# An SSD loop on one Trainium2 core: ScalarE evicts a projection behind the next tile's exponential and rounds weight chunks by halves

## The reference, cut to what matters

```python
lmat = jnp.exp(jnp.where(mask, seg, -jnp.inf))        # seg = a_cs[l] - a_cs[s]
cb = jnp.einsum('bclgn,bcsgn->bcgls', cc, bc)
y_diag = jnp.einsum('bcgls,bcghls,bcsghp->bclghp', cb, lmat, xdt)
states = jnp.einsum('bclgn,bcghl,bclghp->bcghpn', bc, decay_states, xdt)
# scan over chunks: s = s * chunk_decay + states
y_off = jnp.einsum('bclgn,bcghpn,bcghl->bclghp', cc, prev, jnp.exp(a_cs))
```

## Time and profile before

| what | us |
|---|---|
| median of 3 runs | 3088.34 (3086.95 to 3089.32) |
| the profiled execution, its own time | 3097.28 |
| its span, first to last instruction | 3095.4 |
| TensorE busy | 2751.9 (89%) |
| VectorE busy | 1479.2 (48%) |
| ScalarE busy | 964.9 (31%) |
| GpSimd busy | 656.9 (21%) |

### The profile page before, as it was taken

How to read it: one execution, slowest core, us unless ns; L and a number is a source line. 1 busy time by engine, 2 the same in 40 slices (tenths; PEclk the granted TensorE clock), 3 DMA queues, 4 the chain that set the end, 5 groups by cost and what they waited for, 6 DMA issues and landing times.

```text
span 3095.4 us, 34166 instructions
## 1 busy us (share of the span) xinstructions
PE 2751.9 (89%) x13390; PEld 1402.8 (45%) x13390; DVE 1479.2 (48%) x2307; ACT 964.9 (31%) x1115; POOL 656.9 (21%) x202
## 2 busy tenths in 40 slices
PE   5999988886999999998878787778889899999996
PEld 2577655633444444444454433234444444444443
DVE  6145432467444444456554649955324822222225
ACT  2322323223332222224333253315333422222331
POOL 1210111111221122221522121214311722211224
PEclk8999988798999999999878898889999999999998
DMA  8221130021111111110022120011010111111111
GB/s 284 82 69 55 45 109 28 28 79 44 55 41 41 54 54 54 54 60 23 32 78 68 55 95 0 0 41 55 28 41 28 55 55 55 42 39 54 54 42 55
DMA packets 95643, 172.83 MB, mean 56 GB/s; under 512 B 5648, under 2 KB 37792, under 8 KB 94752
## 3 DMA queue, kind: packets, MB, share of 16 engines
q1 hardware_dynamic: 83232, 134.70, 13.3%
q10 hardware_dynamic: 12288, 36.46, 3.3%
HBM read 164.85 MB, written 6.29 MB: 55 GB/s over the span
## 4 chain that ended last, share of the span: by engine, by line
PE 67%; DVE 14%; DVEq 4%; ACT 4%; issue 4%; POOLq 3%; DMA 2%; PEld 1%; ACTq 1%; PEldq 0%; POOL 0%; SPq 0%
PE PS L582 20%; PE PS L583 19%; PE PS L584 19%; DVEq L1867 2%; PE PS L621 2%; DVE XT L1868 1%; PE PS L1271 1%; ACT WS L1338 1%; DVE Hf L1868 1%; ACT WB L1337 1%; DMA Hf<-in_w_ada 1%; PE PS L1244 1%; DVE ST L1888 1%; POOLq L520 1%; POOLq L550 1%
## 5 line engine op out<-in xcount | busy, mean ns | idle before, releaser
L483 POOL TENSOR_TENSOR WB<-WS,WB 128x2048 f16<-128x2048 f32 x108 | 447.9, 4168 | 2077.4 <-ACT WS L1338 2076.9
L582 PE MATMUL PS<-XT,WB 128*128 128x512 f16 (+1 forms) x1584 | 604.3, 381 | 31.1 <-DVE Hf L1866 11.1
L583 PE MATMUL PS<-XT,WB 128*128 128x512 f16 (+1 forms) x1584 | 604.1, 381 | 0.0
L584 PE MATMUL PS<-XT,WB 128*128 128x512 f16 (+1 forms) x1584 | 603.9, 381 | 0.0
L582 PE MATMUL PS<-WB,Hf 128*128 128x512 f16 x1440 | 549.7, 382 | 29.9 <-DVE S L2194 10.7
L583 PE MATMUL PS<-WB,Hf 128*128 128x512 f16 x1440 | 549.1, 381 | 0.0
L584 PE MATMUL PS<-WB,Hf 128*128 128x512 f16 x1440 | 548.7, 381 | 0.0
L1866 DVE CAST Hf<-S 128x512 f16<-128x512 f32 x172 | 158.7, 923 | 547.3 <-ACT S L1568 431.2
L1337 ACT ACTIVATE WB<-WS 128x2048 f16<-128x2048 f32 (+3 forms) x118 | 212.4, 1800 | 468.6 <-PEq L591 461.6
L582 PEld LDWEIGHTS PS<-XT,WB 128*128 128x128 f16 (+1 forms) x1584 | 155.5, 98 | 229.5 <-issue 32.8
L2191 DVE SCALAR_TENSOR_TENSOR R<-PS,R 128x512 f32<-128x512 f32 x176 | 120.9, 691 | 257.9 <-PE PS L584 254.0
(11 more groups left out here) (342 smaller groups left out, 2921.4 us busy)
## 6 DMA issues: line engine op xcount, KB each, us to landing
WS<-in_w_ff SPq DMA_DIRECT2D x32, 1024.0 KB, 5.1
WS<-in_mlp_w SPq DMA_DIRECT2D x32, 1024.0 KB, 5.1
WS<-in_w_in SPq DMA_DIRECT2D x48, 256.0 KB, 4.4
Hf<-in_w_ada ACTq DMA_DIRECT2D x12, 1024.0 KB, 7.6
Hf<-in_w_ada SPq DMA_DIRECT2D x8, 1024.0 KB, 10.4
WS<-in_w_out SPq DMA_DIRECT2D x8, 1024.0 KB, 5.1
WS<-in_w_in SPq DMA_DIRECT2D x14, 512.0 KB, 3.8
R<-in_x SPq DMA_DIRECT2D x4, 1024.0 KB, 10.1
```

Source lines behind the costliest of these rows:

```text
L483: pool.tensor_tensor(WB[:, slot, 1, hf * 2048:(hf + 1) * 2048], WS[:, hf, :], WB[:, slot, 0, hf * 2048:(hf + 1) * 2048], ALU.subtract).the ...
L582: pe.matmul(o, ah, bh, start=(first and k == 0), stop=False, skip_group_check=True)
L583: pe.matmul(o, ah, bl, start=False, stop=False, skip_group_check=True)
L584: mm = pe.matmul(o, al, bh, start=False, stop=(last and k == n - 1), skip_group_check=True)
```

## The change

ScalarE's list alone is changed. The eviction of jobs 0, 1 and 2 moves from t = 1, 3, 5 to t = 2, 4, 6, and so stands behind the exponential of the following tile; job 3 stays at t = 7. The rounding of `wk1` (g = 0) moves from ahead of the loop to its first half behind exp(0) and its second half behind exp(1). The rounding of `ssd1` or `s5rg` moves from behind exp(3) and the eviction of job 1 to its first half behind exp(4) and that eviction, and its second half behind exp(5). The number of instructions is the same, and no other engine's list changes.

```diff
--- before.py
+++ after.py
@@ -1337,9 +1337,12 @@
                 act.activation(WB[:, slot, 0, hf * n:(hf + 1) * n], WS[:, hf, 0:n], ACT.Copy, scale=W_SCALE)
                 act.activation(WS[:, hf, 0:n], WS[:, hf, 0:n], ACT.Copy, scale=W_SCALE).then_inc(w_hi, 1)
 
+            def round_part(c, hf):
+                round_half(c % 2, hf, 4 * narrow.get(c, HALF), loaded_at[c], c + 1)
+
             def round_chunk(c):
                 for hf in range(2):
-                    round_half(c % 2, hf, 4 * narrow.get(c, HALF), loaded_at[c], c + 1)
+                    round_part(c, hf)
 
             act.wait_ge(consts_in, 32)
             act.activation(SM[:, 0:8], col("c", 0, 8), ACT.Silu).then_inc(silu_c, 1)
@@ -1652,22 +1655,21 @@
                 for q in range(2):
                     b = side_in()
                     act.activation(BN[:, q * HALF:(q + 1) * HALF], PS[:, b, :], ACT.Copy).then_inc(evac[b], 1)
-                if g == 0:
-                    round_chunk(C["wk1"])
                 for t in range(TT):
                     K[0] = ssd_side(g, t, "seg")
                     b = side_in()
                     act.activation(WT[t % 2], PS[:, b, :], ACT.Exp)
                     act.drain().then_inc(evac[b], 1)
                     act.sem_inc(ssd_e, 1)
-                    if t % 2:
+                    for i in {2: [0], 4: [1], 6: [2], 7: [3]}.get(t, ()):
                         b = wide_in()
-                        i = t // 2
                         dst = (VE[i % 2][:, (i // 2) * HALF:(i // 2 + 1) * HALF] if g else
                                KE[:, 2 * i:2 * i + 2, :].rearrange("p k m -> p (k m)"))
                         act.activation(dst, PS[:, b, :], ACT.Copy, scale=UNSCALE).then_inc(evac[b], 1)
-                    if t == 3:
-                        round_chunk(C[("ssd1", "s5rg")[g]])
+                    if g == 0 and t < 2:
+                        round_part(C["wk1"], t)
+                    if t in (4, 5):
+                        round_part(C[("ssd1", "s5rg")[g]], t - 4)
                     if t == 7:
                         round_chunk(C[("wv0", "rgg")[g]])
                 act.drain().then_inc(kv_ready, 1)
```

## The result

The changed kernel takes 3067.06 us (median of 5 runs, 3063.34 to 3075.39), and the kernel before, run beside it, 3089.32 us (3086.95 to 3097.17). The ratio is 0.9928, with a 95% interval of 0.9913 to 0.9942: 0.72% faster, 22 us. The forecast was 3075.8 us, and its range, 3065 to 3083.5 us, holds the result. The time is close to that of the first rival (3065.6 us), though.

What follows compares the result with a forecast made beforehand. TensorE, busy in 89% of the span, was the bound, so only its standing time could go. 4.1 + 2.7 + 3.1 + 3 x 0.86 = 12.5 us off 3088.3 gave 3075.8 us, range 3065 to 3083.5 us.

Steps and rivals of the forecast that it cites:

- first rival: After tile 3, LA(6) gets in ahead of GpSimd's second half: gain 7.8 and 8.2 us, 3065.6 us; chance 0.18.
- Where TensorE stood, and for whom: TensorE stood 6.15 us before y(0) and 5.91 us before seg(5), the exponentials coming behind rounded chunks on ScalarE.
- (a): Exponential ahead of eviction, t = 1 to 2 and 5 to 6: 0.86 us each, 2.6 us for three places.
- (b): wk1 rounded by halves in the first group: y(2) comes 4.1 us earlier; bounds 2.3 and 8.4 us.
- (c): ssd1 and s5rg rounded by halves, both groups: y(5) earlier by 2.7 and 3.1 us, despite an 8.1 us pause.
- GpSimd, if asked for first, gets in: I take that: At y(3) + 8.5 us GpSimd's second half goes first; LA(6), 0.2 us too late, stands until it ends.
- second and third rivals: Second: wait only exchanged, 3083.5 us, chance 0.15. Third: TensorE's clock stays down after the pause, 3100 us, chance 0.05.
- (d): Queues behind: SyncE gets wk1's halves back 5.7 us later, everything behind t = 7 stands as before; cost nothing.

Runs made afterwards that it cites:

- second execution: The changed kernel run again with nothing altered: 0.9926 of the kernel before, loops 61.37 and 53.18 us.
- memset kernel: The changed kernel plus three one-column VectorE memsets ahead of LA(6) in each loop: 0.9967 of the kernel before.
- kernel with the short splits: The changed kernel with GpSimd's split of ssd1 and s5rg cut to 64 of 2048 columns, for timing only: 0.9899 of the kernel before.

## Why the prediction was right, and where it was off

The time lies in the range because the range reached down to 3065 us, just past the time of a rival with a chance of 0.18. By its own sign the forecast failed: it was to be wrong if LA(6) took 0.69 us, and LA(6) took 0.69 us in both loops. Loop lengths were to fall by 7.7 and 4.8 us, and fell by 11.0 and 9.1. The closeness to the first rival's time is in part luck too: its parts add up to 22.7 us in the loops, where 20.1 were measured, and 1.9 us lie behind the loops, where neither had any.

- **Where TensorE stood, and for whom:** right, but for one instruction. The waits for ScalarE went where they were said to, and the cost moved to VectorE held by GpSimd, in three of the instructions named: w(1), L2380 of finish(0), L2385 of finish(3) (now L2382 and L2387). The fourth, LA(6), was not held; XD(5) was instead.
- **(a)** 0.86 us a place: 0.83 in the first loop's second place and 0.84 in the second loop's first. The second loop's second place gave 0.19, for there w(6) came late behind XD(5), as the first rival had it.
- **(b)** 4.1 us at y(2): 5.0 (24.96 to 19.92 us). But y(2) to y(3) then took 10.96 us, not 9.34, at the lower clock of the window 1558.0 to 1564.9. Net 3.4. The second execution, with y(0) later, has 4.2 at y(2) and 2.3 net. The pause before cb(3) follows from my own working, and I did not ask the clock about it.
- **(c)** 2.7 and 3.1 us: 6.7 and 7.8. This is the term that was mis-sized, by 8.6 us of the sum, and it is the step "GpSimd, if asked for first, gets in: I take that", with GpSimd put first by 0.2 us. The mechanism and the price of this order were right, as the memset kernel shows. The order was not, and the price of the other was 2.2 us too low at y(5) (Y + 16.2, measured Y + 18.4), for want of the clock's fall. I had GpSimd's first half wait for L2382 to Y + 4.2; it started at Y + 4.05 and ended at Y + 8.12. I had ScalarE resume 0.75 us after an exponential's start; it was 0.83. So LA(6) asked at Y + 8.48, not 8.60, and GpSimd at Y + 8.48, not 8.40. A lead of 0.2 us became none. The rows behind the step (L2380 and L2382) could not tell of this: there GpSimd's second half followed the first at once, and here it came 0.36 us later, when ScalarE had rounded it.
- The Trainium skill (SBUF — State Buffer, Who interferes with whom) has issue order decide who blocks. The memset kernel agrees: its mask started 0.08 us later and was held. In the changed kernel the profile gives mask and half equal starts, so it can't say which was issued first; the half's 4.60 us only show that the mask held it.
- **The first rival** had, with the 0.86 of (a), 8.7 and 9.1 us from y(3) to y(6), 1.0 us lost at y(6) included. Measured are 7.5 (29.20 to 21.70) and 8.0 (29.60 to 21.65). It expected no fall of the clock behind a pause of 4.3 us, and there was one in both loops. Of its 1.0 us at y(6), 0.65 was lost in the second loop and nothing in the first.
- **The second and third rivals** did not come. The clock rose 4.8 us after cb(6) in the first loop and 4.1 in the second, near the forecast's 5.0.
- **(d)** Nothing behind t = 7: right for the stretch between the loops, 60.03 us in both. From the last y(7) to the end there are the 1.9 us of the result's section.
- What the prediction missed in its parts is how they hang together. It priced (a), (b) and (c) as three gains that add up. Alone, (b) and (c) are losses (3.0 and 5.3 us over the two loops), since a half that stands behind a job's eviction keeps the next exponential waiting for the whole job.

## What to carry to other kernels

In an in-order list, an instruction that waits for a long job should stand behind everything that others wait for. Price a move with its neighbours in the list, not alone. And where two engines ask for one thing within 0.2 us of each other, give both outcomes nearly even chances, or move one of them, for the estimate can't be that fine, though the chip's own answer was the same in all six loops that had these starts.

## What the runs showed of the hardware that was not expected

- 0.08 us in the order of two requests was worth 3.8 us in each loop.
- The clock fell 1.1 us behind the end of a wait of 2.4 us (before cb(3)), and in the first loops of two kernels 0.7 and 0.8 us behind the end of a wait of 1.7 us (before y(6)), while the same wait in their second loops brought no fall; so not only with waits of 6 us as in the rows of before.
- Executions of the same code differ ahead of the loops. Two windows of the same stretch, first of before and then of after:

```profile
582.00:609.30 27.30, 27.30 (x120) 17.88 (x119) 7.12 (x40) 0.21 (x1) 0.00 (x0) 0.50 0.00 1
```

```profile
582.00:602.30 20.30, 17.44 (x124) 11.07 (x124) 11.08 (x57) 0.42 (x2) 0.00 (x0) 1.00 0.00 1
```

In the one TensorE was at 1.2 GHz for 27.3 us, busy throughout, and in the other at 2.4 GHz with its work done sooner. Behind it the changed kernel's execution is 11.7 us ahead (VectorE's L1991 at 607.3 us before, the same instruction at 595.6 after). The kernel with the short splits, whose loops are the shortest of all, was at 0.50 there too. That is the main reason why its profiled span, 3064.1 us, is longer than the changed kernel's 3061.0. What makes the clock go one way or the other there was not tried.
